# A two-block transformer on one core: part of the first products at five norm seams made on token halves

## The reference

```python
def modulate(x, g_pre, shift, scale):
    return rms_norm(x, g_pre) * (1 + scale) + shift

def residual_add(x, y, g_post, gate, res_w):
    return x + res_w * (1 + gate) * rms_norm(y, g_post)
...
        h = modulate(x, norm_pre[l, 0], mod[:, 0, 0], mod[:, 0, 1])
        x = residual_add(x, swiglu(h, ffn_w_gate[l, 0], ...), norm_post[l, 0], mod[:, 0, 2], 0.5)
        h = modulate(x, norm_pre[l, 1], mod[:, 1, 0], mod[:, 1, 1])
        y = token_mixer(h, mix_w_in[l], ...)
        x = residual_add(x, y, norm_post[l, 1], mod[:, 1, 2], 1.0)
        h = modulate(x, norm_pre[l, 2], mod[:, 2, 0], mod[:, 2, 1])
        x = residual_add(x, swiglu(h, ffn_w_gate[l, 1], ...), norm_post[l, 2], mod[:, 2, 2], 0.5)
```

## Time and profile before

| | |
|---|---|
| median of 3 runs | 1698.38 us (1696.91 to 1699.64) |
| the profiled execution | 1699.22 us, its span 1697.4 us |
| TensorE busy | 1659.9 us, 98% of the span |
| weight loads | 1550.8 us, 91% |
| VectorE busy | 1266.7 us, 75% |
| ScalarE busy | 873.8 us, 51% |
| mean granted TensorE clock | 0.999 |

### The profile page before, as it was taken

The page is one execution under the profiler, slowest core; times in us unless marked ns, Lnnn a source line. Parts: engine busy times, 40 slices in busy tenths (PEclk is TensorE's granted clock), DMA queues, the critical chain, the costliest instruction groups (busy, mean ns, idle before and its releaser), DMA issues.

```text
span 1697.4 us, 29607 instructions
## 1 busy us (share of the span) xinstructions
PE 1659.9 (98%) x12344; PEld 1550.8 (91%) x12344; DVE 1266.7 (75%) x1852; ACT 873.8 (51%) x1215; POOL 21.7 (1%) x39
## 2 busy tenths in 40 slices
PE   3999999999999999999999999999999999999998
PEld 3999899988999899989999988999899989989997
DVE  7777889987878677676877765887677686778553
ACT  4555466654544365666464334534355676473432
POOL 0000000000000000000000000000000000000000
PEclk9999999999999999999999999999999999999999
DMA  9878756786777745755558786777945846547542
GB/s 377 319 256 253 268 198 218 208 329 244 295 285 277 294 154 195 223 182 207 208 199 286 284 223 237 246 279 288 287 154 199 221 177 224 212 176 259 198 162 100
DMA packets 71079, 398.80 MB, mean 235 GB/s; under 512 B 8225, under 2 KB 8737, under 8 KB 36385
## 3 DMA queue, kind: packets, MB, share of 16 engines
q1 hardware_dynamic: 67968, 387.43, 65.1%
q0 software_dynamic: 2976, 9.47, 1.6%
HBM read 395.79 MB, written 1.08 MB: 234 GB/s over the span
## 4 chain that ended last, share of the span: by engine, by line
PE 83%; DVE 6%; ACT 5%; DVEq 2%; DMA 1%; issue 1%; SPq 1%; ACTq 0%
PE att L695 19%; PE lin L518 18%; PE lin L519 18%; PE lin L520 18%; DVE lo L1312 3%; ACT hi L922 2%; PE att L802 2%; PE lin L558 1%; PE lin L560 1%; PE lin L568 1%; DVEq L1678 1%; PE att L852 1%; DMA ada_s<-in_ada 1%; ACT work L942 1%; PE pt L829 1%
## 5 line engine op out<-in xcount | busy, mean ns | idle before, releaser
L1312 DVE TENSOR_TENSOR lo<-raw,hi 128x2048 fp32r<-128x2048 f32 x269 | 615.5, 2291 | 254.1 <-ACT hi L922 253.4
L518 PE MATMUL lin<-h_hi,hi 128*128 128x256 f32 x2448 | 688.3, 281 | 1.4 <-DVE work L1673 1.0
L520 PE MATMUL lin<-h_hi,lo 128*128 128x256 f32 x2448 | 683.3, 279 | 0.0
L519 PE MATMUL lin<-h_lo,hi 128*128 128x256 f32 x2448 | 683.3, 279 | 0.0
L922 ACT ACTIVATE hi<-raw 128x2048 fp32r<-128x2048 f32 x269 | 513.3, 1912 | 191.4 <-PE att L695 99.6
L518 PEld LDWEIGHTS lin<-h_hi,hi 128*128 128x128 f32 x2448 | 460.1, 188 | 4.1 <-issue 3.9
L519 PEld LDWEIGHTS lin<-h_lo,hi 128*128 128x128 f32 x2448 | 460.3, 188 | 0.1
L520 PEld LDWEIGHTS lin<-h_hi,lo 128*128 128x128 f32 x2448 | 460.1, 188 | 0.0
L1325 DVE CUSTOM_DVE_ANT_0 ada_w<-ada_w,cs 128x1024 f32<-128x1024 f32 x179 | 217.8, 1219 | 11.9 <-DMA ada_w<-in_ada 11.7
L1162 ACT ACTIVATE work<-lin 128x256 f32<-128x256 f32 x88 | 33.8, 384 | 269.2 <-PE lin L520 268.2
L695 PE MATMUL att<-hi,act_lo 128*128 128x512 f32 x440 | 138.8, 389 | 0.0
(11 more groups left out here) (291 smaller groups left out, 2021.9 us busy)
## 6 DMA issues: line engine op xcount, KB each, us to landing
raw<-in_w SPq DMA_DIRECT2D x269, 1024.0 KB, 4.9
ada_w<-in_ada SPq DMA_DIRECT2D x179, 512.0 KB, 5.1
ada_s<-in_ada SPq DMA_DIRECT2D x13, 512.0 KB, 15.1
bias<-in_bias POOLq DMA_DIRECT2D x16, 256.0 KB, 4.5
ffn_row<-rows POOLq DMA_DIRECT2D x5, 512.0 KB, 9.1
x<-in_x SPq DMA_DIRECT2D x1, 1024.0 KB, 9.8
ra<-rows POOLq DMA_DIRECT2D x2, 512.0 KB, 5.2
dcon<-in_dcon SPq DMA_DIRECT2D x1, 896.0 KB, 7.9
```

The source lines that it names most:

```text
L518: mm(out, w_hi, a_hi, start=start, stop=False, skip_group_check=skip)
L519: mm(out, w_hi, a_lo, start=False, stop=False, skip_group_check=skip)
L520: return mm(out, w_lo, a_hi, start=False, stop=stop, skip_group_check=skip)
L1312: tt(lo[SLOT[c]][:], raw[:, c % RAW, :], hi[SLOT[c]][:].bitcast(F32), ALU.subtract).then_inc(*s_lo.up(c))
```

## The change

At the five normed seams only:

- `keep_busy` ahead of the first half's transposes makes 2 products instead of 5; the 4 products ahead of the second half's transposes go.
- As soon as the first half is turned, its 128 columns of `h_hi` are made for six tiles: 0 and 1 by ScalarE, 2 to 5 by VectorE (`first_half_of_h` on both).
- TensorE then makes, for both chunks, the products of these six tiles' first 128 columns with `hi` and `lo` (`into_h_by_halves`): 6 tiles x 2 chunks x 2 column blocks x 2 parts = 48 products of 128 columns. They stand ahead of the second half's transposes.
- After these transposes come the other 128 columns of the six tiles (again 48 products of 128 columns), the products of tiles 6 and 7 with all 256 columns (16), and the 32 with `h_lo` (`fm_second_half`).
- `h_hi` of the second half is made for 128 columns only in tiles 0 to 5. The full tiles in `work`, from which `h_lo` is made, stay.

```diff
+            def half_product(out, j, t, c, a, start):
+                b = slice((j * KT + t) * P, (j * KT + t + 1) * P)
+                o = out[:, j * SEQ + a * P:j * SEQ + (a + 1) * P]
+                mm(o, hi[SLOT[c]][:, b], h_hi[:, t, a * P:(a + 1) * P], start=start, stop=False, skip_group_check=True)
+                mm(o, lo[SLOT[c]][:, b], h_hi[:, t, a * P:(a + 1) * P], start=False, stop=False, skip_group_check=True)
+
+            def into_h_by_halves(tag, buf, n, one, two):
+
+                keep_busy(n)
+                turn_tokens(tag, buf, 0)
+                outs = {}
+                for name in (one, two):
+                    eng.wait_ge(*s_lo.at(AT[name]))
+                    outs[name] = free_bank((AT[name], 0))
+                for t in range(6):
+                    eng.wait_ge(*(s_first_a if t < 2 else s_first_v).at((tag, t)))
+                    for name in (one, two):
+                        for j in range(2):
+                            half_product(outs[name], j, t, AT[name], 0, t == 0 and j == 0)
+                turn_tokens(tag, buf, 1)
+                return outs
+
+            def fm_second_half(tag, outs, one, two):
+
+                for tiles in ((0, 2, 1, 3), (4, 5, 6, 7)):
+                    for name in (one, two):
+                        c = AT[name]
+                        for t in tiles:
...
+                                if t < 6:
+                                    half_product(outs[name], j, t, c, 1, False)
+                                    continue
...
-                into_h(l + ".pre1", flat_f, 5, 4)
-                fm_first(l + ".pre1", f"{l}.moba.q0", f"{l}.moba.k0")
+                outs = into_h_by_halves(l + ".pre1", flat_f, 2, f"{l}.moba.q0", f"{l}.moba.k0")
+                fm_second_half(l + ".pre1", outs, f"{l}.moba.q0", f"{l}.moba.k0")
...
+            def first_half_of_h(tag):
+                shift, g, mods = at_of_norm(tag)
+                eng.wait_ge(*s_mods.at(mods))
+                eng.wait_ge(*s_half_across.at((tag, 0)))
+                for t in (0, 1):
+                    act(h_hi[:, t, 0:P], across(t)[:, 0:P], ACT.Identity, bias=mod[:, shift + t:shift + t + 1],
+                        scale=gain[:, g + t:g + t + 1]).then_inc(*s_first_a.up((tag, t)))
...
                 if normed:
                     factor_of_second_half(post, banks)
+                    first_half_of_h(pre)
                 factor_of_x(pre, post, 1)
...
+            def first_half_of_h(tag, tiles):
+                shift, g, _ = at_of_norm(tag)
+                for t in tiles:
+                    eng.wait_ge(*s_half_across.at((tag, t // 2)))
+                    ts(h_hi[:, t, 0:P], across(t)[:, 0:P], gain[:, g + t:g + t + 1], mod[:, shift + t:shift + t + 1],
+                       ALU.mult, ALU.add).then_inc(*s_first_v.up((tag, t)))
...
+                if pre and normed:
+                    first_half_of_h(pre, (2, 3))
                 if pre:
                     half_of_x(pre)
+                    if normed:
+                        first_half_of_h(pre, (4, 5))
                     scaled_x(pre, buf, 1)
```

More of the change, by code:

```diff
@@ L409, in across, with by_halves, at_of_norm @@
             return turned_at[t // 2][:, t % 2 * SEQ:(t % 2 + 1) * SEQ]
+        def by_halves(tag):
+            return tag[1:] in (".pre1", ".pre2") or tag == "1.pre0"
+        def at_of_norm(tag):
+            l, n = int(tag[0]), int(tag[-1])
+            return ADA_ONCE + ADA_LAYER * l + 24 * n, 16 + 24 * l + 8 * n, f"{l}.{n}"
         def bank_of(unit):
@@ new lines, in fm_second_half @@
+            def fm_second_half(tag, outs, one, two):
[3 more added lines that the diff above has]
+                        for t in tiles:
+                            if name == one:
+                                eng.wait_ge(*(s_h_hi_v if t in (2, 3) else s_h_hi).at((tag, t)))
+                            for j in range(2):
+                                if t < 6:
+                                    half_product(outs[name], j, t, c, 1, False)
+                                    continue
+                                b = slice((j * KT + t) * P, (j * KT + t + 1) * P)
+                                o = outs[name][:, j * SEQ:(j + 1) * SEQ]
+                                mm(o, hi[SLOT[c]][:, b], h_hi[:, t, :], start=False, stop=False, skip_group_check=True)
+                                mm(o, lo[SLOT[c]][:, b], h_hi[:, t, :], start=False, stop=False, skip_group_check=True)
+                for name in (one, two):
+                    c = AT[name]
+                    for t in (4, 5, 6, 7, 0, 1, 2, 3):
+                        if name == one:
+                            eng.wait_ge(*s_h.at((tag, t)))
+                        for j in range(2):
+                            b = slice((j * KT + t) * P, (j * KT + t + 1) * P)
+                            ins = mm(outs[name][:, j * SEQ:(j + 1) * SEQ], hi[SLOT[c]][:, b], h_lo[:, t, :], start=False,
@@ L1003, in h_first, with from_x @@
                 eng.wait_ge(*s_mods.at(mods))
-                def from_x(out, t):
+                left = slice(P, SEQ) if by_halves(tag) else slice(0, SEQ)
+                def from_x(out, t, tokens=slice(0, SEQ)):
                     eng.wait_ge(*s_across.at((tag, t // 2)))
-                    return act(out, across(t), ACT.Identity, bias=mod[:, shift + t:shift + t + 1],
+                    return act(out, across(t)[:, tokens], ACT.Identity, bias=mod[:, shift + t:shift + t + 1],
                                scale=gain[:, g + t:g + t + 1])
                 for t in (0, 1):
-                    from_x(h_hi[:, t, :], t).then_inc(*s_h_hi.up((tag, t)))
+                    from_x(h_hi[:, t, left], t, left).then_inc(*s_h_hi.up((tag, t)))
                 for t in (6, 7):
@@ L1017, in h_first @@
                         eng.wait_ge(*s_scaled.at((tag, t)))
-                    act(h_hi[:, t, :], turned_tile(t), ACT.Copy).then_inc(*s_h_hi.up((tag, t)))
+                    tokens = left if t < 6 else slice(0, SEQ)
+                    act(h_hi[:, t, tokens], turned_tile(t)[:, tokens], ACT.Copy).then_inc(*s_h_hi.up((tag, t)))
                 for t in (0, 1, 2, 3):
@@ L1399, in modulated, with from_x @@
                     shift = ADA_ONCE + ADA_LAYER * int(tag[0]) + 24 * int(tag[-1])
-                def from_x(out, t):
+                left = slice(P, SEQ) if by_halves(tag) else slice(0, SEQ)
+                def from_x(out, t, tokens=slice(0, SEQ)):
                     eng.wait_ge(*s_across.at((tag, t // 2)))
-                    return ts(out, across(t), gain[:, g + t:g + t + 1], mod[:, shift + t:shift + t + 1],
+                    return ts(out, across(t)[:, tokens], gain[:, g + t:g + t + 1], mod[:, shift + t:shift + t + 1],
                               ALU.mult, ALU.add)
                 for t in (2, 3):
-                    from_x(h_hi[:, t, :], t).then_inc(*s_h_hi_v.up((tag, t)))
+                    from_x(h_hi[:, t, left], t, left).then_inc(*s_h_hi_v.up((tag, t)))
                 for t in (4, 5):
```

17 lines of the change are left out of this document (13 added, 4 removed).

## The result

| | before | changed |
|---|---|---|
| median | 1698.83 us (1696.91 to 1699.64, 4 runs) | 1708.53 us (1708.31 to 1708.74, 4 runs) |
| ratio | | 1.0061, 95% interval 1.0046 to 1.0076 |
| span of the profiled execution | 1697.4 us | 1706.5 us |

The changed kernel is 0.6% slower: 9.7 us by the medians. The forecast was 1707.0 us, +8.6.

What follows compares the result with a forecast made beforehand. The prediction took TensorE, busy 98% of the span, as the bound. A seam changes by 96p − 8.84 us, +1.72 at p = 0.11; five give +8.6 on 1698.38, so 1707.0 us, with 1690 to 1720 to hold 8 in 10.

Steps and rivals of the forecast that it cites:

- TensorE has no slack behind a seam: At the seams, what a seam gains or loses goes into the end time in full.
- First transposes 1.29 us earlier: At each changed seam, fewer constant products let the first half's transposes start at 605.92 instead of 607.21.
- This gain is real, and it needs no product on halves.: Claim that the first transposes' 1.29 us a seam comes from fewer constant products alone.
- p = 0.11 us from the weight load: Start-to-start price of a 128-column product at the seams, bound by its load's 0.108 us; range 0.108 to 0.117.
- The nearest row that the prediction leaned on: Profile records of plain f32, 128 x 128 weights and 128 moving columns, 0.11 us apart, taken as support for p.
- Second transposes at 612.48: At 0.pre1, they start when the first 48 narrow products end, 2.3 us later than before.
- 1.08 us from there to the first product: At 0.pre1, time from second transposes to the first product behind them, 1.245 us before the change.
- The next chunk 19.6 us behind the last product: Window of each of the five seams, growing from 17.9 to about 19.6 us.
- The scaling 0.35 us late: VectorE's scaling of the second half, behind its new tiles, comes at 610.55 instead of 610.20.
- The first rival: At the seams, loads hide and columns count: p below 0.092, at 0.062 a seam gains 2.3 us, 1687 us; chance 0.20.
- The cover that I named at nothing for the splits: VectorE's and ScalarE's splits of the next two chunks stay covered by TensorE waits; otherwise up to 1 us a seam.
- The clock: Rival at the seams: a new wait or a 1.2 GHz stretch doubling some of 5 us, to 1730 us; chance 0.05.

Runs made afterwards that it cites:

- three_tiles: The changed kernel with narrow products for tiles 0 to 2 only, the rest multiplied 256 columns at a time; 1695.48 us, ratio 0.9987 to the kernel before.
- fill_2_7: The kernel before with 2 constant products instead of 5 ahead of the first transposes, 7 instead of 4 ahead of the second; 1698.99 us against 1698.29, ratio 1.0002.
- halves_fill_5: The changed kernel with 5 constant products ahead of the first half's transposes, as before the change; 1714.64 us, ratio 1.0098 to the kernel before.
- weights_64: The changed kernel with each narrow product loading 64 weight columns instead of 128, still moving 128; 1695.72 us, ratio 0.9985 to the kernel before.
- moving_64_three: three_tiles with 64 moving columns instead of 128 in its narrow products; 1707.73 us against 1700.44 for the kernel before, ratio 1.0039.
- moving_64: The changed kernel with each narrow product moving 64 columns instead of 128, same 128 x 128 weights; 1753.95 us, ratio 1.0326 to the kernel before.
- values_first: three_tiles at FFN seams; at the two before the mixers, moba.v0 first with 12 full-width first-half products between the transposes; 1694.10 us, ratio 0.9975 to the kernel before.
- fill_2_0: The kernel before with 2 constant products instead of 5 ahead of the first transposes and none ahead of the second; 1705.02 us, ratio 1.0040.

## Why the prediction was right, and where it was not

- *TensorE has no slack behind a seam.* Right: 9.6 us more in the five windows, 9.7 us more by the medians. An agreement as close as this, and that of 1707.0 with 1708.5, is in part luck: one stretch between two seams takes 1.1 us more or less in the same code (`three_tiles`).
- *First transposes 1.29 us earlier.* Right (2.38 to 1.09). At the two seams behind the out-projection 1.27 and not 1.09 after the last product, since there the operand comes first at that time; I took the five as alike, which is good to 0.2 us.
- *"This gain is real, and it needs no product on halves."* Wrong: `fill_2_7` has it and is as fast as before. The second half's operand sets the seam, as the prediction's own reading of the timeline had it. The 1.29 us counted in the changed kernel only because the narrow products had made TensorE late; `halves_fill_5` shows both.
- *p = 0.11 us from the weight load.* Right: 0.112, and `weights_64` against `moving_64_three` shows that the load sets it. The nearest row that the prediction leaned on, plain f32 records with 128 columns 0.11 us apart, agreed by luck: with 256 columns such records are 0.216 us apart, so there the columns set the price and not the load. The Trainium skill's 81 ns for N = 128 ("TensorE: Matmul & The Clock Gate", section "Back-to-back issue gap") are not met here. Its load time of columns over 1.2 (section "LDWEIGHTS (loading the stationary operand)"), 107 ns for 128 columns, agrees with 0.112 us within 5%. For 64 columns it gives 53 ns, near the 0.060 us; but there the 128 moving columns, 0.055 us by the prediction's rows, could set the price as well, and no run separates the two.
- *Second transposes at 612.48, 7.65 us behind the last product.* Measured 7.63. *1.08 us from there to the first product*: 1.02. *The next chunk 19.6 us behind the last product*: 19.76. The 0.15 us are 96 x 0.002 = 0.19 for the narrow products and 0.13 for the rest behind the second transposes (a step of 0.17 instead of 0.117 us where narrow ones give way to wide ones, 617.96 to 618.13, twice a seam, and the rounding of 5.60), less 0.06 for the first product and less 0.12 because the first narrow product came at 2.25 us and not at 2.37. Per seam +1.87 instead of +1.72: this is what was mis-sized.
- *The scaling 0.35 us late*: it wasn't; VectorE's tiles of 128 columns took 0.36 us and not nearly 0.5. It would have changed nothing.
- *The first rival's price.* Its condition didn't come up, and its 1687 us was wrong. `weights_64` has p = 0.06. The 15.6 us that the rival's sum gives a seam is what the two seams before the mixers take (15.36, 15.39), but the three FFN seams wait 2.2 us for VectorE, 6.6 us in all, and the clock falls behind each: 1695.7 us. (In that sum the first 48 end at 610.7; from tile 5 at 609.9 and 8 x 0.062 it would be 610.4. The second transposes came at +5.68 to +5.82, which is 610.5 to 610.65.) The cover that I named at nothing for the splits was 0.2 us thick on the gain's side.
- *The clock.* Rightly left out for this change (1.00 over all windows). But I had priced its fall as a part of 5 us; `moving_64` shows 17 to 20 us of it at a seam, and `weights_64` 3.4 us behind a wait of 2.2.

So the cause is this. A first-half product of 128 columns costs 0.112 us and its second half again 0.112, where the whole costs 0.117. What is done ahead in this way saves 0.005 us of what comes later, and the gap between the first half's tiles and the second half's operand holds 3.1 us of it. The change put 5.4 us there.

## What to carry to other kernels

Work that is split to fill a gap pays only if the second piece becomes cheaper: ask what a piece costs at its new size, with its weight load, before asking whether it fits. If the load is as long as the stream, cut along the stationary operand and not along the moving one: then half of the work is half as many products at full width, as with the tokens stationary in `values_first`. And know the width of the gap: up to it even useless pieces cost nothing (`fill_2_7`), beyond it everything ahead of them on that engine counts too (`halves_fill_5`).

## What the runs showed of the hardware

- An fp32r product with 128 x 128 weights starts 0.112 us after the one before with 64 and with 128 moving columns, 0.117 with 256; with 64 weight columns and 128 moving ones 0.060.
- In the same code the ordinary products, 128 x 128 weights and 256 moving columns, come 0.1167 or 0.1178 us apart on average over some 125 us behind a seam, with TensorE never idle. The changed kernel's trace has both, at different seams. The cause is open.
- The granted clock fell to 1.2 GHz for 3.4 us after TensorE had idled 3.0 to 3.2 us (`fill_2_0`, five seams of five), and also after it had idled 2.2 us (`weights_64`, three of three, behind narrow products). It also fell with TensorE never idle, behind 3 to 5 us of products with 64 moving columns, and for 17 to 20 us; with 128 moving columns over the same 5.4 us (the changed kernel) it stayed at 2.4 GHz. What the chip looks at to decide this, these runs don't settle.
